# Forms of the first up pairs begun inside the last output projection tile, the norm's sum and roots behind later products, and the residual stored in quarters

## The reference

```
def conv_ffn(h, w_up, conv_w, conv_b, w_down):
    up, gv = jnp.split(h @ w_up, 2, axis=-1)
    up = causal_dwconv(up, conv_w, conv_b)
    return (jax.nn.gelu(up) * gv) @ w_down
...
        x = x + jnp.concatenate([y_gla, y_s5, y_rg], axis=-1) @ w_out[l]
        h = rmsnorm(x, mlp_norm[l])
        x = x + conv_ffn(h, w_up[l], mlp_conv_w[l], mlp_conv_b[l], w_down[l])
```

## Time and profile before

| | |
|---|---|
| median of three runs | 2292.95 us (2292.47 to 2293.45) |
| the profiled execution | 2293.18 us, of which its span is 2291.2 us |
| mean granted TensorE clock | 0.959 |
| busy: TensorE | 2108.1 us, 92% of the span |
| busy: VectorE, GpSimd, ScalarE | 57%, 52%, 29% |

### The profile page before, as it was taken

One profiled execution on the slowest core, in us unless ns is written; L12 is line 12 of the kernel. 1 busy time (PEld: TensorE's weight loads), 2 busy tenths in 40 slices (PEclk: granted clock), 3 DMA queues, 4 the chain that ended last, 5 costly groups with the idle time before them and its releaser, 6 DMA issues.

```text
span 2291.2 us, 26391 instructions
## 1 busy us (share of the span) xinstructions
PE 2108.1 (92%) x9832; PEld 1645.0 (72%) x9832; DVE 1308.3 (57%) x1929; ACT 665.4 (29%) x1144; POOL 1193.3 (52%) x737
## 2 busy tenths in 40 slices
PE   6999989987975999996898998998899999999997
PEld 4888889986843666664674556687688888878885
DVE  7998335664231322225788876757666666664334
ACT  4110057667221111112320024223444444430101
POOL 3553245761637658003017850324799999943353
PEclk9999999989997999998999998998999999999998
DMA  5653165664457778326423211312122222271322
GB/s 215 218 221 120 46 163 150 181 178 162 147 209 265 289 296 329 118 83 239 161 74 110 83 46 37 120 67 71 55 83 83 83 83 83 83 284 55 116 78 101
DMA packets 87171, 319.97 MB, mean 140 GB/s; under 512 B 25048, under 2 KB 26328, under 8 KB 78872
## 3 DMA queue, kind: packets, MB, share of 16 engines
q1 hardware_dynamic: 48616, 206.67, 25.8%
q10 hardware_dynamic: 30880, 73.02, 9.1%
q0 software_dynamic: 7552, 38.60, 4.6%
HBM read 229.59 MB, written 96.53 MB: 142 GB/s over the span
## 4 chain that ended last, share of the span: by engine, by line
PE 58%; DVE 10%; POOL 4%; issue 3%; DMA 3%; ACT 2%; SPq 0%; DVEq 0%; ACTq 0%; POOLq 0%
PE ps L1623 5%; PE ps L1146 5%; PE ps L1625 5%; PE ps L1624 5%; PE ps L1150 5%; PE ps L1148 5%; PE ps L1400 4%; PE ps L1384 2%; PE ps L1380 2%; PE ps L1382 2%; PE ps L1381 2%; PE ps L1304 1%; PE ps L1368 1%; PE ps L1162 1%; PE ps L1164 1%
## 5 line engine op out<-in xcount | busy, mean ns | idle before, releaser
L1146 PE MATMUL ps<-work_part 128*128 128x512 f32 x976 | 308.3, 397 | 11.4 <-POOL work_part L876 9.7
L1150 PE MATMUL ps<-work_part 128*128 128x512 f32 x976 | 302.0, 391 | 0.0
L872 POOL CAST work_part<-ring 128x1024 fp32r<-128x1024 f32 (+3 forms) x80 | 81.2, 1014 | 397.8 <-PE ps L1150 273.8
L1625 PE MATMUL ps<-work_part 128*128 128x512 f32 x572 | 224.4, 392 | 0.0
L1146 PEld LDWEIGHTS ps<-work_part 128*128 128x128 f32 x976 | 183.6, 189 | 55.7 <-POOL work_part L876 7.5
L1150 PEld LDWEIGHTS ps<-work_part 128*128 128x128 f32 x976 | 184.2, 189 | 38.9
L1148 PE MATMUL ps<-hT_part,work_part 128*128 128x512 f32 x672 | 208.4, 392 | 0.0
L1623 PE MATMUL ps<-work_part 128*128 128x512 f32 x440 | 175.5, 399 | 15.1 <-DVE hT L3092 5.3
L876 POOL TENSOR_TENSOR work_part<-ring,work_part 128x1024 fp32r<-128x1024 f32 (+3 forms) x80 | 177.9, 2224 | 12.4 <-PE ps L1598 6.1
L1624 PE MATMUL ps<-work_part 128*128 128x512 f32 x440 | 173.1, 393 | 0.0
L1148 PEld LDWEIGHTS ps<-hT_part,work_part 128*128 128x128 f32 x672 | 127.0, 189 | 26.8
(11 more groups left out here) (451 smaller groups left out, 4646.7 us busy)
## 6 DMA issues: line engine op xcount, KB each, us to landing
pages<-w_moe SPq DMA_DIRECT2D x16, 2048.0 KB, 9.3
w_parts<-work_part SPq DMA_DIRECT2D x36, 512.0 KB, 3.6
work_part<-w_parts SPq DMA_DIRECT2D x36, 512.0 KB, 4.1
pages<-w_moe SPq DMA_DIRECT2D x16, 1024.0 KB, 6.5
x_slots<-zeros ACTq DMA_DIRECT2D x31, 512.0 KB, 4.2
work<-x_slots ACTq DMA_DIRECT2D x31, 512.0 KB, 5.7
y_slots<-work ACTq DMA_DIRECT2D x31, 512.0 KB, 2.7
ring<-w_in_units SPq DMA_DIRECT2D x24, 512.0 KB, 3.7
```

Source lines behind the costliest of these rows:

```text
L1146: pe.matmul(ps[:, c], whi[:, w], hi[k][:, c], start=(k == 0), stop=False)
L1150: mm = pe.matmul(ps[:, c], wlo[:, w], hi[k][:, c], start=False, stop=(k == len(hi) - 1))
L1625: mm = pe.matmul(bank_, wlo[:, cols], xhi, start=False, stop=(k == 3), skip_group_check=joined)
```

## The change

Six things change in the lists, and nothing in the arithmetic.

1. **Last projection tile.** last_mix_tile takes the 16 products of weight highs by MIX_LO first and signals (lows), then for each k high by high and low by high, and signals after k = 3 (heads).
2. **ScalarE and VectorE.** ScalarE makes k = 0 to 2 of the highs of b0 and b1 after "lows", and those of t2 and t3 after "heads". VectorE puts one norm addition and the lows k = 0 to 2 of b0, b1 and t3 ahead of its addition of tile 7, and the eighth norm addition behind the last lows.
3. **The norm.** Its sum stands behind P6 and the spreading of the roots behind P1 of pair 1. The sums and roots use halves of PSUM slots that the pairs do not use (MLP_SUMS, MLP_ROOTS), the diagonals the tile YUP[1] (MLP_DIAG). VectorE inverts after up_second; scaling by RB comes after the gate sum.
4. **ScalarE behind P5.** Two highs of pair 1's weights, the copy of P6, the root, the highs of t4, the other highs of pair 1 (they stood behind the t4 highs), then the copy of the roots.
5. **SyncE and GpSimd.** The load of pair 1 is issued before the store of Hp[7]. GpSimd makes s2's low between the third and fourth low of t2, and its sums for pair 1 wait for the seventh norm addition and no longer for the spread roots.
6. **The residual of the first block** is stored with four transfers of two tiles each; VectorE waits for a quarter ahead of the low that overwrites its first tile.

The diff, cut to its core (left out are waits that only follow from it: those of f_loaded, of pair 1 on TensorE, of the sums for pair 1 on GpSimd, and of the reload of h):

```
...
         PRODUCTS.append(("P4", FF - 1))
+        PRODUCTS = ["lows", "heads"] + PRODUCTS
         product_count = {p: PRODUCTS0 + n + 1 for n, p in enumerate(PRODUCTS)}
+        MLP_SUMS = PS[(b0_ + 3) % SLOTS][:, HALF:HALF + NT]
+        MLP_ROOTS = [PS[(b0_ + 1) % SLOTS][:, HALF:S], PS[(b0_ + 3) % SLOTS][:, HALF:S]]
+        MLP_DIAG = YUP[1]
...
                 for m in range(8):
+                    if m == 7:
+                        load_pair(1)
                     park_h(m)
...
                         load_pair(0)
-                load_pair(1)
                 for j in range(2, FF):
...
                     sp.wait_ge(ysum_ready, NT)
-                    sp.dma_start(h_keep, hT[:]).then_inc(parked, 16)
+                    for i in range(4):
+                        sp.dma_start(h_keep[:, 2 * i:2 * i + 2, :], hT[:, 2 * i:2 * i + 2, :]).then_inc(x_loaded[i], 16)
                 if u == U_OUT2 + RING:
...
             pair_combine(0)
-            for v in LO_ORDER[:3]:
-                pair_low(0, v)
-            for k in range(4):
+            def t2_low(k):
                 hi, lo, whole = x_of("t2", k)
...
                 pool.tensor_tensor(lo, whole, hi.bitcast(f32), ALU.subtract).then_inc(x_lo["t2"][0], 1)
-            for v in LO_ORDER[3:]:
+            for v in LO_ORDER[:3]:
+                pair_low(0, v)
+            for k in range(3):
+                t2_low(k)
+            pair_low(0, "s2")
+            t2_low(3)
+            for v in LO_ORDER[4:]:
                 pair_low(0, v)
...
                        [(rest_lo_ready, c + 1) for c in range(4)] + [(heads_lo_ready, h + 1) for h in range(4)], order)
-            for m in range(2, 8):
+            for m in range(2, 7):
                 parts_tile(U_OUT2 + m, P_OUT2 + m, MIX_HI, MIX_LO)
+            def last_mix_tile():
+                ps = slot(P_OUT2 + 7)
+                parts_ready(U_OUT2 + 7)
+                whi, wlo = wparts(U_OUT2 + 7)
+                halves = [slice(half * HALF, (half + 1) * HALF) for half in range(2)]
+                for k in range(NT):
+                    for c in halves:
+                        mm = pe.matmul(ps[:, c], whi[:, k * P:(k + 1) * P], MIX_LO[k][:, c], start=(k == 0), stop=False)
+                mm.then_inc(products_done, 1)
+                for k in range(NT):
+                    w = slice(k * P, (k + 1) * P)
+                    for c in halves:
+                        pe.matmul(ps[:, c], whi[:, w], MIX_HI[k][:, c], start=False, stop=False)
+                    for c in halves:
+                        mm = pe.matmul(ps[:, c], wlo[:, w], MIX_HI[k][:, c], start=False, stop=(k == NT - 1))
+                    if k == 3:
+                        mm.then_inc(products_done, 1)
+                mm.then_inc(mm_done, 1)
+            last_mix_tile()
...
+            def mlp_sum():
+                pe.wait_ge(h_ready, 16)
+                pe.wait_ge(sq_added, n_mlp["add0"] + 7)
+                for tt in range(NT):
+                    mm = pe.matmul(MLP_SUMS[:, tt:tt + 1], n_mlp["scratch"][0][:, tt * P:(tt + 1) * P], ones[:, 0:1],
+                                   start=True, stop=True)
+                mm.then_inc(sums_ready, 1)
+            def mlp_root():
+                pe.wait_ge(inverse_ready, n_mlp["index"] + 1)
+                for half in range(2):
+                    mm = pe.matmul(MLP_ROOTS[half], ones, second(MLP_DIAG, half), start=True, stop=True)
+                mm.then_inc(root_spread, 1)
             p1(0)
...
             p2(0)
-            norm_sum(n_mlp)
             p6(0)
-            norm_root(n_mlp)
+            mlp_sum()
             p3(0)
...
                 p1(j)
+                if j == 1:
+                    mlp_root()
                 p4(j - 1)
...
                         pair_high(0, v)
+                    act.wait_ge(products_done, product_count["lows"])
+                    for i, v in enumerate(("b0", "b1")):
+                        for k in range(3):
+                            x_high(v, k, second(Hp[4 + k], i), 4 + k)
+                    act.wait_ge(products_done, product_count["heads"])
+                    for v in ("t2", "t3"):
+                        for k in range(3):
+                            x_high_turn(v, k)
                     act.wait_ge(mm_done, done(P_OUT2 + 7))
-                    for k in range(3):
-                        x_high("b0", k, second(Hp[4 + k], 0), 4 + k)
+                    pair_high(0, "s2")
+                    act.wait_ge(h_ready, 16)
+                    x_high("b0", 3, second(Hp[7], 0), 7)
+                    x_high_turn("t2", 3)
+                    x_high("b1", 3, second(Hp[7], 1), 7)
+                    pair_high(0, "s4")
+                    x_high_turn("t3", 3)
                 mlp_square(t)
...
                     x_high_turn("t1", t - 1)
-            x_high("b0", 3, second(Hp[7], 0), 7)
-            for k in range(4):
-                x_high_turn("t2", k)
-            for k in range(4):
-                x_high("b1", k, second(Hp[4 + k], 1), 4 + k)
-            for v in HI_ORDER[4:]:
-                pair_high(0, v)
+            pair_high(0, "s3")
...
-            act.activation(root_of_eps[:, n_mlp["index"]:n_mlp["index"] + 1], epsc[:], ACT.Sqrt)
-            norm_std(n_mlp)
-            for k in range(4):
-                x_high_turn("t3", k)
             def copy_p1(j):
...
             copy_p5(0)
+            act.wait_ge(*past(x_lo["b1"], 4))
+            act.wait_ge(sq_ready, n_mlp["sq0"] + 8)
+            for v in HI_ORDER[:2]:
+                pair_high(1, v)
+            copy_u2(0)
+            act.wait_ge(sums_ready, n_mlp["index"] + 1)
+            act.wait_ge(inverse_ready, n_mlp["index"] - 3)
+            act.activation(std[:, n_mlp["index"] % 4, :], MLP_SUMS, ACT.Sqrt, bias=epsc[:], scale=1.0 / D).then_inc(std_ready, 1)
+            for k in range(4):
+                x_high_turn("t4", k)
+            for v in HI_ORDER[2:]:
+                pair_high(1, v)
             act.wait_ge(root_spread, n_mlp["spread"] + 1)
-            act.activation(RB, PS[bank(n_mlp["root_use"])][:, :], ACT.Copy).then_inc(roots_copied, 1)
-            copy_u2(0)
-            for k in range(4):
-                if k % 2 == 0:
-                    act.wait_ge(sums_ready, n_mlp["index"] + 1)
-                x_high_turn("t4", k)
+            for half in range(2):
+                copied = act.activation(second(RB, half), MLP_ROOTS[half], ACT.Copy)
+            copied.then_inc(roots_copied, 1)
             for j in range(FF):
...
                                              op0=ALU.mult, op1=ALU.mult).then_inc(hn_ready, 1)
-                if k == 0:
-                    dve.wait_ge(parked, PARKED + 16)
-                else:
+                if k >= 1:
+                    if k % 2 == 1:
+                        dve.wait_ge(x_loaded[k // 2], 32)
                     dve.wait_ge(hn_ready, k)
...
             for m in range(8):
+                if m == 7:
+                    norm_add(n_mlp, 6)
+                    for v in ("b0", "b1"):
+                        for k in range(3):
+                            x_low_h(v, k)
+                    for k in range(3):
+                        x_low("t3", k)
                 dve.wait_ge(mm_done, done(P_OUT2 + m))
...
                     dve.wait_ge(h_ready, 8 + m + 1)
-                if m >= 2:
+                if 2 <= m < 7:
                     norm_add(n_mlp, m - 1)
...
                     x_turn_234(m - 4)
-            for k in range(3):
-                x_low_h("b0", k)
             dve.wait_ge(h_ready, 16)
...
             x_low_h("b0", 3)
+            x_low_h("b1", 3)
+            x_low("t3", 3)
             norm_add(n_mlp, 7)
-            for k in range(4):
-                x_low_h("b1", k)
...
+            def mlp_inverse():
+                r = std[:, n_mlp["index"] % 4, :]
+                dve.wait_ge(std_ready, n_mlp["index"] + 1)
+                link(dve.reciprocal(r, r))
+                dve.wait_ge(*past(h_parked, 16 * 8))
+                dve.tensor_tensor(MLP_DIAG.rearrange("p (t n) -> p t n", n=P), r.unsqueeze(2).to_broadcast([P, NT, P]),
+                                  ident.unsqueeze(1).to_broadcast([P, NT, P]), ALU.mult).then_inc(inverse_ready, 1)
             up_first(0)
-            norm_inverse(n_mlp)
-            dve.wait_ge(roots_copied, 3)
-            dve.wait_ge(*past(up_sums, 1))
-            up_scale(0, 0)
-            for k in range(4):
-                x_low("t3", k)
+            up_second(0)
+            mlp_inverse()
             for k in range(4):
                 x_low("t4", k)
-            up_second(0)
+            up_gate(0)
+            dve.wait_ge(roots_copied, 3)
+            dve.wait_ge(*past(up_sums, 3))
+            up_scale(0, 0)
             up_scale(0, 1)
-            up_gate(0)
             up_conv(0)
...
```

14 lines of the change are left out of this document (4 added, 10 removed).

## The result

| | before | after |
|---|---|---|
| median | 2293.23 us (10 runs) | 2279.86 us (10 runs) |
| ratio to before | | 0.9945, 95% interval 0.9934 to 0.9957 |
| span of the profiled execution | 2291.2 us | 2277.8 us |
| first product of pair 0 (P1) starts | 1576.60 us | 1574.18 us |
| from P1 to P4 of pair 0 | 44.40 us | 36.08 us |

The kernel is faster by 0.55% (12.6 us by the ratio, 9.9 to 15.1), against a forecast of 2282.8 us. A second set of runs of the same kernel gave 0.9948 (0.9931 to 0.9965).

The account below looks back on a forecast made before the run. It took the start of P4 of pair 0, after the seam before the up projection, to carry the end: 2293.18 - 2.8 (quarters) - 7.4 (seam) = 2283.0, median 2282.8 us; own range 2280.5 to 2285.5, whole range 2279.5 to 2288.0.

Parts of the forecast that it names:

- Part one, minus 2.8: Start of the second block: storing the residual in quarters removes VectorE's wait, 2.8 us gained, bounds 0 and 2.8.
- Tile 7 at +10.2: Last projection tile: nine lows, four at 1.70 and five at 0.65 us, delay tile 7's addition from 1578.0 to 1586.8.
- The strict reading: Lows ahead of tile 7: GpSimd's four pieces end 1.6 us later, one more low is slow; sum 2283.7 us.
- P2's last quarter at +13.2 and P6 at +16.25: Seam after tile 7: P2's last quarter starts about 1589.8, P6 at 1592.85, 2.9 us earlier than before.
- The norm's sum at 2.4 GHz: Behind P6: the sum's 16 short matmuls take 1.84 us at 2.4 GHz, ending at 1599.7.
- The rival of a low clock through sum and P3: Behind P6: sum costs 3.54 us (plus 1.7), P3 5.1 (plus 2.4), total 2286.9 us; chance 0.15.
- P4 at +37.0: End of VectorE's list after P3: P4 starts at 1613.6 instead of 1621.0, minus 7.4 us.
- P4 at 1.2 GHz again, no gain: P4 of pair 0: after a 3.4 us wait it again runs 4.4 us at 1.2 GHz, so nothing gained.
- the rival with the chance of 0.12: P4 of pair 0 keeps 2.4 GHz because its wait is 1.9 us shorter: minus 2.2 us, 2280.6 us; chance 0.12.
- What is late next: nothing near: After P4: the next pair's weights load behind P4 as before, at the same distance.
- no wait worth naming: TensorE from 1621 on, in the kernel before: no notable wait, so what P4's start gains, the end gains.
- each microsecond there moves P6 and P4: Lows ahead of tile 7's addition, 10.05 us: every microsecond there shifts P6 and P4; slower-kernel chance 0.03.

Follow-up runs that it names:

- GpSimd's t2 lows late: Changed kernel with GpSimd starting its t2 lows and s2 low only once tile 7 is added; 2279.04 us, 0.9938 of the kernel before.
- six lows moved behind tile 7: Changed kernel with inverse and t4 lows ahead of up_second, then b1 and t3 lows behind tile 7, norm's sum behind P3; 2279.42 us, 0.9949 of before.
- the norm alone: Changed kernel with no b0, b1, t2 or t3 work begun ahead of tile 7, norm's move and quarters kept; 2282.61 us, 0.9947 of before.
- the forms alone: Changed kernel with norm's sum, root product and ScalarE's copies at old places, highs and lows still begun early; 2283.69 us, 0.9957 of before.
- one moved line: Changed kernel with up_second moved behind the inverse and the four t4 lows in VectorE's list; 2276.39 us, 0.9920 of before.
- the changed kernel with one store: Changed kernel with the residual stored by one 4 MB transfer again; 2286.57 us (0.9973 of before), second set 2284.15 us (0.9961).

## Why the prediction was right

The time, 2279.86 us, is 2.9 us below the forecast. It lies inside the whole range (2279.5 to 2288.0) by 0.4 us, and outside the range that the forecast gave for itself (2280.5 to 2285.5). By its steps, in the profile:

- **Part one, minus 2.8.** Measured 2.74 (3.88 instead of 6.62), the quarters landing after a median of 10.3 us each. The bound was set too tight: the same wait was 3.6 us long in another profile.
- **Tile 7 at +10.2.** It was +10.0. The lows ahead of it took 8.20 and 1.89 us; the first six hold four at 1.70 and two at 0.65 (8.1), as forecast. GpSimd's four pieces took 7.2 us (1572.18 to 1579.40) instead of 6.4. The strict reading of the Trainium skill, "SBUF — State Buffer", section "Who interferes with whom", by which the two engines exclude each other for whole instructions, would have added 1.6 us to GpSimd's pieces and made one more low slow (11.1 us in all). The trace stands between: GpSimd lost half of that, and no fifth low was slow.
- **P2's last quarter at +13.2 and P6 at +16.25.** +13.1 and +15.9. ScalarE's row from tile 7 to the copy of P1 took 5.8 us (1584.25 to 1590.05) against 6.0.
- **The norm's sum at 2.4 GHz.** 2.02 us, mostly: the clock came back during it. The rival of a low clock through sum and P3 is refuted, here and in every variant with the sum behind P6 (1.84 to 2.20).
- **P4 at +37.0.** +36.1. The diagonal took 1.59 us where 2.3 was put down. GpSimd was at work beside it, as I had assumed, and the row of 2.3 was still not its length; in the variants the same instruction took 1.29 to 2.29 with GpSimd at work beside it in all or part, and no run shows what decides.
- **P4 at 1.2 GHz again, no gain.** Wrong in this profile: 0.50 before, 1.00 after, 2.2 us. It was the rival with the chance of 0.12, priced right. But in the second set P4 had a mean clock of 0.67 with nearly the same wait, so it is no property of the change but luck of this execution: see below.
- **What is late next: nothing near.** Correct: no wait of TensorE over 0.7 us appears until +459. The waits from there on, 2.2, 2.3 and 5.0 us, are in the kernel before too (2.3, 2.3 and 5.0), where the prediction's "no wait worth naming" left them out.
- **Two small slips.** One more low at 1.70 instead of 0.65 adds 1.05 us, so the strict reading gives 2283.9 and not 2283.7; and the chances that count as faster add up to 0.93, not 0.92.

The sum: P1 starts 2.4 us earlier, of the 2.74 gained at the start of the second block; P1 to P4 is 8.3 us shorter; and from P4 to the end it is 2.7 us less (667.5 instead of 670.2), 2.05 of it because P4's twelve matmuls took 2.87 us instead of 4.92. The profiled spans differ by 13.4 us. With P4 at 1.2 GHz, as forecast, the profiled execution would have come out at about 2282 (an estimate: 2279.81 plus 2.05), inside the forecast's own range.

The path was right: tile 7, ScalarE's row, P6, the norm's sum, P3 and VectorE's tail end in P4 as forecast. The run with GpSimd's t2 lows late shows the same chain: the norm's sum starts 2.3 us earlier there and P4 2.7. Two things the prediction did not see. First, its one cost, the nine lows ahead of tile 7, buys no earlier P4 in this order of VectorE's list: without them P4 starts at +35.9. The norm's move and the t3 lows' leaving their late place carry the 8.3 us, and how much each of the two carries, no run shows. Second, the walk started VectorE anew at P3's end and so passed over the 6.9 us that VectorE stands there. And "each microsecond there moves P6 and P4" was too simple. With GpSimd late tile 7 was added 4.1 us earlier, P6 started 1.5 us earlier and P4 2.7; with six lows moved behind tile 7 it was 4.9, 4.9 and 1.1 us. What one microsecond does depends on whether the work is gone or only comes later.

## What to carry to other kernels

When two edits shorten the same stretch, their gains need not add (here 8.5 and 5.3 us gave 8.3). Ask of each variant what holds the end of the stretch: here it was VectorE's full list with the norm alone, TensorE's own row with the forms alone, and the wait for P3 with both. Then put instructions whose inputs are ready into the wait that is left, which here cost one moved line and gave a further 1.8 us of P4's start. A wait for a transfer of fixed length is as long as the work ahead of it is short, so take its price from more than one profile.

## What the runs showed of the hardware

**The same wait can keep or lose TensorE's clock.** After waits of 2.62 to 2.90 us ahead of P4 the first 4.4 us of P4 ran at a granted clock of 1.00, 0.67, 0.50 and 1.00 in four profiles with the same order there:

```profile
1618.30:1622.70 4.40, 4.40 (x10) 3.45 (x11) 2.95 (x4) 2.52 (x2) 0.45 (x1) 0.50 0.00 0
```

```profile
1616.10:1620.50 4.40, 4.40 (x13) 3.56 (x14) 2.96 (x4) 2.52 (x2) 0.45 (x1) 0.67 0.00 0
```

(the changed kernel with one store after a wait of 2.71 us, and the changed kernel's second set after 2.62). After 3.60, 4.32 and 5.32 us it was 0.50, after 2.15 us 0.61, after 1.00 and 1.41 us 1.00. Over P4's twelve matmuls the difference between the two levels is 2 us (4.92 us before, 2.87 after), so a single profile's span carries an error of that size.

**VectorE beside GpSimd.** A 512-column low is 0.65 us with GpSimd quiet and 1.70 beside it; sums that take one operand from PSUM stay at 0.68 in both. Not every instruction beside a working GpSimd pays the full price: the diagonal took between 1.29 and 2.29 us, and the four t3 lows with the norm alone took 5.77 us, 1.4 each. Holding GpSimd back moved the slow operations rather than removing them: the nine lows gained 4.1 us, and the turns and lows behind them lost it again.
